# Four norm seams and the attention steps of a two-block decoder kernel: leading products ahead of the second half's turn, value products beside the scores

## The reference

```python
# first block: two layers
for i in range(2):
    h = rms_norm(x, norm_mix[i])
    x = x + (short_conv_pool_mixer if i == 0 else sparse_attn_conformer_mixer)(h, ...)
    x = x + swiglu(rms_norm(x, norm_ffn[i]), ffn_gate[i], ffn_up[i], ffn_down[i])   # width 2816
# second block: one layer
hn = rms_norm_2(x, ln_g)
proj = hn @ w_in          # q, k, v and gates of three branches, and three gates of width 1024
# branch a: 8 heads; branch b: 3 groups of 8 heads, combined by their softmax weights;
# branch c: 8 heads on 2 key heads, with sinks; all with a relative bias
x = x + sum(sigmoid(gates) * (branches @ w_branch)) @ w_out
```

## Time and profile before

| | us |
|---|---|
| median of three runs | 994.49 |
| the profiled execution | 996.31 |
| its span, first to last instruction | 994.4 |
| PE busy | 972.7 |
| DVE busy | 608.2 |
| ACT busy | 484.9 |
| POOL busy | 213.2 |
| granted TensorE clock, mean | 0.993 |

### The profile page before, as it was taken

The page is one execution under the profiler, slowest core; times in us unless marked ns, Lnnn a source line. Parts: engine busy times, 40 slices in busy tenths (PEclk is TensorE's granted clock), DMA queues, the critical chain, the costliest instruction groups (busy, mean ns, idle before and its releaser), DMA issues.

```text
span 994.4 us, 17117 instructions
## 1 busy us (share of the span) xinstructions
PE 972.7 (98%) x7057; PEld 867.0 (87%) x7057; DVE 608.2 (61%) x827; ACT 484.9 (49%) x726; POOL 213.2 (21%) x178
## 2 busy tenths in 40 slices
PE   9999999999998988999999999999999999999998
PEld 8989999999887877799999997887787888999996
DVE  5866554545488788665444446756464745856654
ACT  5446434343445364753343436456455545647451
POOL 0005970000032140000000000313543604920100
PEclk9999999999999999999999999999999999999999
DMA  8664656555557421356565663645354535553361
GB/s 267 219 217 143 216 175 205 170 199 180 179 158 238 134 99 44 127 180 202 171 208 169 204 218 128 212 169 170 127 170 165 174 129 170 170 189 111 127 211 43
DMA packets 119636, 168.75 MB, mean 170 GB/s; under 512 B 5556, under 2 KB 88596, under 8 KB 119572
## 3 DMA queue, kind: packets, MB, share of 16 engines
q1 hardware_dynamic: 118992, 167.55, 50.8%
q10 hardware_dynamic: 580, 0.30, 0.1%
HBM read 165.38 MB, written 2.46 MB: 169 GB/s over the span
## 4 chain that ended last, share of the span: by engine, by line
PE 84%; DVE 7%; ACT 3%; POOL 2%; issue 2%; SPq 1%; DMA 1%; DVEq 0%; ACTq 0%; POOLq 0%
PE ps L465 24%; PE ps L466 24%; PE ps L467 24%; PE ps L847 2%; DVE scratch_sb L1459 2%; PE ps L874 2%; PE ps L861 2%; DVE wlo_sb L445 1%; SPq L1268 1%; POOL b_inv_sb L2403 1%; PE ps L518 1%; PE ps L687 1%; PE ps L2027 1%; ACT whi_sb L422 1%; DVE nmax_sb L943 1%
## 5 line engine op out<-in xcount | busy, mean ns | idle before, releaser
L445 DVE TENSOR_TENSOR wlo_sb<-raw_sb,whi_sb 128x2048 fp32r<-128x2048 f32 x143 | 331.8, 2322 | 210.5 <-ACT whi_sb L422 210.2
L422 ACT ACTIVATE whi_sb<-raw_sb 128x2048 fp32r<-128x2048 f32 x143 | 273.8, 1916 | 186.2 <-PE ps L467 163.2
L465 PE MATMUL ps<-hhi_sb,whi_sb 128*128 128x256 f32 x1008 | 282.8, 281 | 1.7 <-ACT scratch_sb L2154 1.3
L467 PE MATMUL ps<-hhi_sb,wlo_sb 128*128 128x256 f32 x1008 | 281.4, 279 | 0.0
L466 PE MATMUL ps<-hlo_sb,whi_sb 128*128 128x256 f32 x1008 | 281.3, 279 | 0.0
L465 PEld LDWEIGHTS ps<-hhi_sb,whi_sb 128*128 128x128 f32 x1008 | 189.5, 188 | 4.1 <-issue 2.7
L466 PEld LDWEIGHTS ps<-hlo_sb,whi_sb 128*128 128x128 f32 x1008 | 189.4, 188 | 0.9
L467 PEld LDWEIGHTS ps<-hhi_sb,wlo_sb 128*128 128x128 f32 x1008 | 189.4, 188 | 0.0
L465 PE MATMUL ps<-whi_sb,hhi_sb 128*128 128x512 f32 (+2 forms) x304 | 121.1, 398 | 0.9 <-DVE wlo_sb L445 0.9
L466 PE MATMUL ps<-wlo_sb,hhi_sb 128*128 128x512 f32 (+2 forms) x304 | 117.9, 388 | 0.0
L467 PE MATMUL ps<-whi_sb,hlo_sb 128*128 128x512 f32 (+2 forms) x304 | 117.8, 388 | 0.0
(11 more groups left out here) (333 smaller groups left out, 1349.7 us busy)
## 6 DMA issues: line engine op xcount, KB each, us to landing
raw_sb<-w_in SPq DMA_DIRECT2D x45, 1024.0 KB, 5.0
raw_sb<-ffn_gate SPq DMA_DIRECT2D x22, 1024.0 KB, 5.1
raw_sb<-ffn_up SPq DMA_DIRECT2D x22, 1024.0 KB, 5.1
raw_sb<-ffn_down SPq DMA_DIRECT2D x22, 1024.0 KB, 4.8
raw_sb<-w_in_even SPq DMA_DIRECT2D x8, 1024.0 KB, 9.2
raw_sb<-w_in_odd SPq DMA_DIRECT2D x8, 1024.0 KB, 5.2
raw_sb<-w_branch SPq DMA_DIRECT2D x6, 1024.0 KB, 4.9
scratch_sb<-bias_rows_dram SPq DMA_DIRECT2D x40, 128.0 KB, 3.0
```

Of the source, the lines that this page charges most:

```text
L422: nc.scalar.activation(place(whi, n0), in_raw(n0), ACT.Copy).then_inc(hi_ready, 1)
L445: nc.vector.tensor_tensor(place(wlo, n0), in_raw(n0), place(whi, n0).bitcast(F32), ALU.subtract).then_inc(lo_ready, 1)
L465: nc.tensor.matmul(dst, l_hi, r_hi, start=first, stop=False)
L467: return nc.tensor.matmul(dst, l_lo, r_hi, start=False, stop=last)
```

## The change

Three things are changed. `norm_pe` of the second token half waits for each column half by itself (a new semaphore `xn1_tail` for DVE's half). At the four seams the high by high products of the second weight tile for the first token half (`first_lead`) stand in front of that turn, and the rest of them (`led`) behind it. And value products are moved ahead: in the first attention to the steps that have scores, in the second block's steps in front of the transposes.

```diff
+        def first_lead(pe, e, n, k0, dst, i, first):
+            width = dst.shape[1]
+            hi, _ = w_parts(n, TILE // width)
+            tok, at = slice(i * P, i * P + P), h_count(e, i) + k0
+            pe.wait_ge(hi_ready, n + 1)
+            for k in range(TILE // width):
+                pe.wait_ge(h_hi, at + k + 1)
+                nc.tensor.matmul(dst, hhi[:, k0 + k, tok], hi[:, k, :], start=(first and k == 0), stop=False)
...
-        def first_part(pe, e, n, k0, dst, i, first, last, late):
+        def first_part(pe, e, n, k0, dst, i, first, last, late, led=False):
...
-                pe.wait_ge(h_hi, at + k + 1)
-                nc.tensor.matmul(dst, hhi[:, k0 + k, tok], hi[:, k, :], start=(first and k == 0), stop=False)
+                if not led:
+                    pe.wait_ge(h_hi, at + k + 1)
+                    nc.tensor.matmul(dst, hhi[:, k0 + k, tok], hi[:, k, :], start=(first and k == 0), stop=False)
...
-            pe.wait_ge((xn_ready, xn1_ready)[i], 2 * e + 1 if i else e + 1)
+            pe.wait_ge((xn_ready, xn1_ready)[i], e + 1)
...
+                if e and i and k == 4:
+                    pe.wait_ge(xn1_tail, e)
...
                     first_part(pe, 2 * l + 1, n, 0, ps[:, 4, 0:FFC], 0, True, True, False)
+                    first_lead(pe, 2 * l + 1, n + 1, 0, ps[:, 5, 0:FFC], 0, True)
                     norm_pe(pe, 2 * l + 1, 1)
-                    first_part(pe, 2 * l + 1, n + 1, 0, ps[:, 5, 0:FFC], 0, True, True, True)
+                    first_part(pe, 2 * l + 1, n + 1, 0, ps[:, 5, 0:FFC], 0, True, True, True, True)
...
+            if m >= 1:
+                pair_pv(pe, jobs, p0, 2 * m - 2)
+                pair_pv(pe, jobs, p0, 2 * m - 1)
             if 0 <= 2 * m < len(jobs) // 2:
                 pair_t(pe, jobs, p0, 2 * m)
                 pair_t(pe, jobs, p0, 2 * m + 1)
-            if m >= 1:
-                pair_pv(pe, jobs, p0, 2 * m - 2)
-                pair_pv(pe, jobs, p0, 2 * m - 1)
...
-        TURN_STEP, VALUE_STEP = range(1, 30, 4), [*range(6, 31, 4), 32]
+        TURN_STEP, VALUE_STEP = range(1, 30, 4), range(4, 33, 4)
```

More of the change, by code:

```diff
@@ L324, in build @@
         sq_sum, rms_inv = sem("sq_sum"), sem("rms_inv")
-        xn1_ready, rows_done = sem("xn1_ready"), sem("rows_done")
+        xn1_ready, xn1_tail, rows_done = sem("xn1_ready"), sem("xn1_tail"), sem("rows_done")
         xn_ready, xn_T, h_hi, h_lo = sem("xn_ready"), sem("xn_T"), sem("h_hi"), sem("h_lo")
@@ L663, in norm_dve @@
                 dve.wait_ge(rms_inv, NT * e + 2)
-                nc.vector.tensor_scalar(xn[:, 1, 512:D], x[:, 1, 512:D], sinv[:, 1:2], None, ALU.mult).then_inc(xn1_ready, 1)
+                nc.vector.tensor_scalar(xn[:, 1, 512:D], x[:, 1, 512:D], sinv[:, 1:2], None, ALU.mult).then_inc(xn1_tail, 1)
                 split_lo(dve, STAGES[e] + 1)
@@ L1019, in mix1_pe @@
             first_part(pe, 2, QT, 0, ps[:, 4, :], 0, True, False, False)
+            first_lead(pe, 2, QT + 1, 4, ps[:, 4, :], 0, False)
             norm_pe(pe, 2, 1)
-            first_part(pe, 2, QT + 1, 4, ps[:, 4, :], 0, False, True, True)
+            first_part(pe, 2, QT + 1, 4, ps[:, 4, :], 0, False, True, True, True)
             first_part(pe, 2, QT, 0, ps[:, 5, :], 1, True, False, False)
@@ L1970, in blk2_pe @@
                     t, i = e[2] - N_B2, e[4]
-                    first_part(pe, 4, e[2], 4 * t, ps[:, bank(e[1][3] + i), :], i, t == 0, t == 1, t == 1)
-                    if (e[2], e[4]) == (N_B2, 0):
+                    first_part(pe, 4, e[2], 4 * t, ps[:, bank(e[1][3] + i), :], i, t == 0, t == 1, t == 1,
+                               (t, i) == (1, 0))
+                    if (t, i) == (0, 0):
+                        first_lead(pe, 4, N_B2 + 1, 4, ps[:, bank(e[1][3]), :], 0, False)
                         norm_pe(pe, 4, 1)
```

## The result

The kernel after takes 990.62 us (median of 5 runs, 988.24 to 991.77), the kernel before 995.05 (994.39 to 996.18): a ratio of 0.9946, 95% interval 0.9929 to 0.9964, or 5.4 us less (the two medians are 4.4 apart). In a later group of runs the ratio was 0.9963 (0.9949 to 0.9976), 3.7 us. The forecast was 993.0, no difference that can be told; the kernel is faster, and the time is at the lower edge of the range.

A forecast was written before the change was run, and what follows sets the result against it. PE's instruction issue was taken as the bound (busy 972.7 of 994.4 us). Seams 0.8, second block 0.2 and first attention 0.5 sum to 1.5 us off the 994.49 median: 993.0 us, range 990.6 to 995.3.

The forecast's parts named there:

- The seams: Four seams: leading products in front of the turn fill PE's stalls, gaining 0.36 + 0 + 0.28 + 0.14 = 0.8 us.
- The change of form: Second block's steps on PE: the new order saves 0.20 us in steps 1 and 2, 2.2 us if PE bounds everything.
- The later transposes: Second block: DVE's shift waits longer, making PE late by 0.43 us in unit 3, 1.08 in unit 4; block nets +0.2.
- The first attention: End of the first attention: earlier value products let L1588 start sooner, 1.15 - 0.6 = 0.5 us gain.
- a late L1577: First attention: value products ahead of transposes at 380 make DVE's L1577 wait some 0.6 us, taken off the 1.15 gain.
- The step that failed: Second block, units 1, 2 and 5: chains have slack or barely move, so only the steps' 0.44 us each is gained.
- A: Second block: chains in units 3 and 4 have slack, so steps give their full 2.2 us: 991.0 us; chance 0.20.
- B: Wait at 851.9 grows and may bring one more clock fall, costing 1.7 us: 994.7 us; chance 0.16.
- C: Second block: form change saves nothing, two new waits lower the clock: 998.0 us, 996.7 with one fall; chance 0.07.
- D: Seams only move PE's wait from the turn to L528 and the steps cancel: no gain, 994.5 us; chance 0.07.

The follow-up runs named there:

- seams_only: The kernel before with the seams' part alone (leading products before the turn, wait per column half): 993.84 us, ratio 0.9995 to before.
- after_again: The kernel after, unchanged, run again in a later group: 990.25 us, ratio 0.9963 to the kernel before.
- pool_late: The kernel after plus one small POOL write ahead of its scalings in the first unit's last k: 991.66 us, ratio 0.9978 to the kernel before.
- values_only: The kernel before with only the steps of the first attention's value products changed (VALUE_STEP): 993.32 us, ratio 0.9989 to before.
- steps_only: The kernel before with only the second block's steps reordered, value products in front of transposes: 991.78 us, ratio 0.9964 to before.
- dve_late: The kernel before plus one small DVE instruction in front of the L445 at 701.8 us: 994.17 us, ratio 0.9998 to before.
- unit4_back: The kernel after with transposes first again in the fourth unit's step 2 only: 989.88 us, ratio 0.9954 to the kernel before.
- seam2_hold: The kernel after with POOL's three L1715 behind the second seam held until DVE's L445 is done: 987.59 us, ratio 0.9931 to the kernel before.
- dve_later: The kernel before plus three small DVE instructions in front of the L445 at 701.8 us: 991.74 us, ratio 0.9973 to before.

## Why the prediction was wrong, point by point

**The seams: right.** In the profile, gains of 0.31, 0, 0.22 and 0.13 us where 0.36, 0, 0.28 and 0.14 were forecast, and at the second seam the idle moved from the turn to L539. What limits that seam I had half right: L445, but a slowed one. The wait per column half was not tried by itself, and the times can't tell the seams' gain from 0 (seams_only, -1.4 to +0.4).

**The change of form: right.** In the second unit the value products stand behind the scores at 0.22 us by these rows:

```profile
720.02 0.28 PE L861 MATMUL ps<-qkh_sb,qkl_sb 64*128 64x128 f32 x2
720.24 0.69 PE L888 MATMUL ps<-scratch_sb 128*64 128x64 f32 x16
720.85 1.09 PE L875 MATMUL ps<-ident_sb,scratch_sb 128*128 128x128 f32 x8
721.70 0.48 PE L465 MATMUL ps<-whi_sb,hhi_sb 128*128 128x512 f32 x1
722.02 0.39 PE L466 MATMUL ps<-wlo_sb,hhi_sb 128*128 128x512 f32 x1
```

The price that no row of before had was taken as 0.21. From the last scores to the second weight product it is 722.02 - 720.02 = 2.00, forecast 1.99; units 1, 2 and 5 gave 0.44, 0.44 and 0.45 for 0.44.

**The later transposes: right in unit 4, right in size and wrong in place in unit 3.** POOL's root of the fourth unit starts at 831.71, 1.1 us later against PE's products than before, and PE's idle grew from 0.41 to 1.51 us. In unit 3 the loss, a step of +0.49 in the starts where 0.43 was forecast, came in front of L465, which waited for a PSUM bank:

```profile
782.91 0.50 PE L465 MATMUL ps<-whi_sb,hhi_sb 128*128 128x512 f32 x1 [0.22 <-DVE qkl_sb L2304]
```

DVE's L2304 comes behind the later shift. (The idle shown is shorter than the stall.) POOL's chain, which I had named, was not late in the end: its scalings,'s 3.02 us, took 2.27, since L445 met them at another point.

**The first attention: right in mechanism, a term mis-sized.** L1588 (now L1603) follows DVE's taps without a wait, as forecast:

```profile
389.34 2.04 DVE L1474 SCALAR_TENSOR_TENSOR scratch_sb<-scratch_sb,vec_sb 128x256 f32<-128x256 f32 x4
391.30 0.68 DVE L1603 TENSOR_TENSOR ylo_sb<-ps,yhi_sb 128x512 fp32r<-128x512 f32 x1
```

The 0.6 us that I took off for a late L1577 was too much. From DVE's L438 to this instruction it is 391.84 - 379.46 = 12.38 us before, and as much in the five experiments with the old order. With the new order it is 391.30 - 380.15 = 11.15 in the kernel after, after_again and pool_late, and 11.43 to 11.49 in the five others, whose L1577 is late by 0.3. So the end of that stage gave 0.9 to 1.2 and not 0.5; values_only's 1.1 agrees, with an interval that holds 0.5 as well. In the profile it shows as 0.80 in all, since more of the stage ran at the low clock: 13.7 us where it was 10.2.

**The step that failed** is the sentence "In units 1, 2 and 5 I find the chains with over 1 us of slack or started by step 3, whose copies move under 0.1". The copies moved as little as it says: in steps_only they start 1.00 us earlier than before (692.17 for 693.17) and PE's products 0.91, so by 0.09. What did not follow is that 0.09 us has no price. The runs show 3.55 us at that place, and -3.6 us for steps_only, where the second block's steps stood at 0.2. I read the 1.9 us wait as the end of a chain of fixed durations. Its last link was 4.12 us for two instructions that take 2.05 in unit 4, and I did not ask why:

```profile
840.83 2.05 POOL L2411 TENSOR_TENSOR scratch_sb<-scratch_sb,b_inv_sb 128x512 f32<-128x512 f32 x2
```

The rows for the answer were in the trace: L445 begins 0.08 us ahead of the second scaling. That place could give 0 to 3.6 us, which by my other terms makes 989.4 to 993.0.

**The rivals.** A (chains have slack, 991.0) has the right time for another reason: unit 4 did lose its 1.1 us. B and C added falls of the clock; unit 4's longer wait brought none in the traces, and the fall at 705 went. C also needed a form change that saves nothing. (Its two times do not match: 998.0 takes 1.6 us for that and 996.7 takes 2.0; with 1.6 the case of one fall is 996.3.) D fell with the first and third seam, whose stalls went in the profile.

**What stays open.** With the chance of a fall behind the wait (below) the parts of my account (seams, end of the first attention, the units' steps, the wait at 705, the low clock behind it) sum to 0.7 + 0.9 to 1.2 + 0.3 + 1.9 + 1.0 = 4.8 to 5.1 us, and measured were 5.4 and 3.7. How much of the scatter is the clock in the first attention I can't split: its low stretches lay elsewhere in nearly every profile.

## What to carry to other kernels

Ask of every instruction on a waiting chain whether it is as long as its like elsewhere; one that is twice as long may have a neighbour that holds it up, and then any change that shifts the two by a tenth of a microsecond may give or take the whole difference. Where POOL works on a chain that PE waits for, hold DVE's long two-input instructions that nobody needs soon behind it by a wait: that gave 2.9 us here for one wait, and does not hang on 0.01 us as the kernel after does. A table of start differences between two traces names the place of a gain at once, and is worth making before any experiment.

## What was not expected of the hardware

- The first to start won, down to hundredths. With L445 0.08 us (before, seams_only, values_only) or 0.03 us (pool_late) ahead POOL's scaling took 3.11 to 3.16 us, and it ended 0.90 us behind L445's end each time. With L445 0.01 us behind (the kernel after, twice) L445 took 3.17. Where the records have the scaling 0.002 to 0.003 us ahead it fell either way: DVE first in dve_late, POOL first in steps_only, unit4_back and seam2_hold.
- DVE's instructions in a row can keep POOL out for more than one of them: a copy of POOL took 4.19 us at 309.90 in the kernel after, through the last three taps, an L445 and two L1488, and its twin of the same size 0.46 us behind them.
- Not every instruction of DVE does this: POOL's L2411 at 683.6 in the kernel before took 1.04 us beside two L886, which have one operand in PSUM. But one SBUF input is no sign of safety: L675, which reads one wide tile from SBUF, took 0.88 us beside POOL and 0.48 without it, and dve_later's third small instruction 1.02 for 0.17.
- The same wait of 1.9 us (2.0 in dve_late) brought the clock down in three profiles (before, values_only, dve_late) and not in two (seams_only, pool_late). Behind it in seams_only:

```profile
704.70:708.00 3.30, 3.30 (x16) 2.68 (x15) 1.80 (x3) 2.88 (x3) 3.14 (x4) 1.00 0.73 276
```

A fall costs about 1.7 us here and is not a fixed part of a wait's price; I counted it as a chance of 3 in 5, from these five profiles alone. What decides it these runs do not show.
